# Samples' attention over a paged cache: queries spread by GpSimd copies, a page over 64 partitions, page tables loaded ahead

## The chip, the core and the metric

The kernel runs on one core of one Trainium2 chip. Its time is the device time of one execution in microseconds (us), as the median of several runs. A core has a matmul engine (TensorE, PE in the rows), a vector engine (VectorE, DVE), an activation engine (ScalarE, ACT), a general one (GpSimd, POOL) and a queue engine (SyncE, SP) that issues most DMAs. Each runs its own list of instructions in order, and they meet at semaphores. SPq and ACTq in the rows are the instructions that issue DMAs.

## The reference

One step of a two-layer decoder: a convolution layer and an attention layer, both with an MLP, for one prompt of 512 tokens and eight samples of eight tokens. All is float32. The change touches the samples' attention in the second layer, which reads a cache of latents and rotary keys through a table of pages:

```python
past_c = cache_kv_latent[page_table].reshape(DB, past_len, KV_LORA)      # 8 samples, 2048 keys, 512
past_kr = cache_k_rope[page_table].reshape(DB, past_len, QK_ROPE)        # 64
...
def sample_attention(q_lat, q_rope, past_c, past_kr, c, kr):
    s_past = latent_scores(q_lat, q_rope, past_c, past_kr)
    s_new = latent_scores(q_lat, q_rope, c, kr)
    s_new = jnp.where(jnp.tril(jnp.ones((T, T), dtype=bool)), s_new, -jnp.inf)
    p = jax.nn.softmax(jnp.concatenate([s_past, s_new], axis=-1), axis=-1).astype(c.dtype)
    return (jnp.einsum('bqhk,bkc->bqhc', p[..., :P], past_c)
            + jnp.einsum('bqhk,bkc->bqhc', p[..., P:], c))
```

A sample has 16 pages of 128 keys; eight heads of eight tokens make 64 queries.

## The kernel before, in words

The work on the two groups goes on together until the prompt's attention is done (eight heads, `hd`, with four blocks of queries each). Then comes the stage in question: a loop over the eight samples `i`. A sample is two units `u` = 2i and 2i + 1 of eight pages, and a unit two halves `s` of four pages.

**Loads.** `cache_loads` is SP's program. A unit's latents go to one of four places in `HELD` (`half_pages`), its ropes to one of four in `ROPES`; so unit u can be loaded only when unit u - 4 has been read (`unit_read`). Page `q` of a half goes to partitions 32q to 32q + 31, four keys in each (8 KB of latents, 1 KB of ropes): per unit 8 + 8 DMAs, ordered latents, ropes, latents, ropes by half. `pages_of` loads a sample's row of the page table into `table` by a DMA and waits for it; `page(n)` reads one number of it into a register (`value_load`, L490). Units 0 to 3 are loaded in code that is written out and has its own waits for buffers of the stage before; units 4 to 15 in a loop `Fori(1, NS // 2)` over pairs of samples. Both DMAs of a half raise one semaphore (`half_landed`).

**Turning.** DVE transposes blocks of 32x32, so that the channels lie on the partitions: `turn_pages` (L2376, half a unit) and `turn_ropes` (L2382, half a unit) into `TURN[u % 2]`, that is `TURNED` or `Y`.

**Queries.** The scores read `Q4[0]`: 18 blocks of 64 queries by 32 channels on partitions, each of the four 32-partition groups with the channels in another order. `QLAT` and `QRS` hold all samples' queries. `queries(i)`, on ACT, copies sample i's by 18 DMAs: 16 from 32 partitions of `QLAT` to 32 others (L1394), two for the ropes (L1396). Sample 0's go into `Q4[0]`, all others into `Q4[1]`, and GpSimd copies `Q4[1]` to `Q4[0]` (L1752) when the sample before has been scored. GpSimd also copies the queries for the new keys to `QS` (L1747, L1749).

**The order in a sample.** PE's `sequence`: scores of unit u (L3092 from `TURNED`) and of u + 1 (L3092 from `Y`), turning the weights (`turn`, L3099), `give` (L3127, the sample before), values of u (L3112), turn, the swap (L3153), the new keys of the next sample (L3080, L3082), values of u + 1. ACT's: `weigh` of the sample before (L1423), `weights` (the exponentials, L1430) and `turned_weights` (L1445) for u and u + 1, then `queries(i + 2)`. DVE's: `unit_top(u)` (L2405), pages of u + 2, `unit_top(u + 1)`, ropes of u + 2, half the pages of u + 3, `unit_sum` (L2417, L2420), `keep`, `gain_output(u)` (L2428), the rest of u + 3, `finish` (L2440 to L2453; its L2446 waits for ACT's L1423), `new_top(i + 1)` (L2391, L2393), for which PE's second scores wait.

**Sample 0.** At the end of the prompt's last head PE waits for `q4_in`, sample 0's 18 DMAs, before its new keys (L3080), since these read the ropes from `Q4[0]`; behind them in PE's list stand the last head's turn (L3053, after DVE's L2338, after ACT's L1368, after DVE's L2329) and its output (L3063). ACT issues the DMAs before that L1368. After the stage PE goes on with the products of `wo` (L2557).

Of the kernel before, what the change touches and what calls it, by code (L numbers as in the profile page):

```python
# [39 lines left out]
NS, TQ = 8, 8  # L40
# [221 lines left out]
def decoder_step(nc, io):  # L262
    with ExitStack() as ctx:
# [168 lines left out]
        CHUNKS = 4  # L432
        OUTS = 3
        MERGES = 5
        Q4_LOADS = 18
# [12 lines left out]
        def half_ropes(u, s):  # L448

            return ROPES[u % 4][:, 256 * s:256 * s + 256]  # L450
# [7 lines left out]
        table_in, keys_turned, score_mm, unit_read, q4_in, csn_mm = (  # L458
            sem("table_in"), sem("keys_turned"), sem("score_mm"), sem("unit_read"), sem("q4_in"), sem("csn_mm"))
# [12 lines left out]
        table = sb("table", [1, PAGES], I32)  # L472
# [3 lines left out]
        def half_landed(u, s):  # L476

            return pages_in[u % 4][s], 128 * (u // 4 + 1)

        def cache_loads(sp):  # L480

            def pages_of(sample):

                sp.dma_start(table[:], io["page_table"][sample, :]).then_inc(table_in, 16)
                sp.wait_ge(table_in, 16)
                sp.sem_clear(table_in)
# [5 lines left out]
            def load_latents(u, s, pages):  # L492

                dst = half_pages(u, s).rearrange("p (a c) -> p a c", a=1)
# [5 lines left out]
            def load_ropes(u, s, pages):  # L500

                dst = half_ropes(u, s).rearrange("p (a c) -> p a c", a=1)
                for q in range(4):
                    sp.dma_start(dst[32 * q:32 * q + 32],  # L504
                                 io["cache_k_rope"].rearrange("n (p k) c -> p n (k c)", k=4)[:, bass.ds(pages[q], 1)])\
                        .then_inc(half_landed(u, s)[0], 16)

            pages_of(slice(0, 1))
# [3 lines left out]
            pages = [page(q) for q in range(16)]  # L512
            for s in range(2):
                load_latents(0, s, pages[4 * s:4 * s + 4])
            sp.wait_ge(kvt_done, NH)
            sp.wait_ge(v_mm, NH // 2)
            for s in range(2):
                load_ropes(0, s, pages[4 * s:4 * s + 4])
            for s in range(2):
                load_latents(1, s, pages[8 + 4 * s:12 + 4 * s])  # L520
                load_ropes(1, s, pages[8 + 4 * s:12 + 4 * s])
            pages_of(slice(1, 2))
            pages = [page(q) for q in range(16)]
            for s in range(2):
                load_latents(2, s, pages[4 * s:4 * s + 4])
            sp.wait_ge(pe_read_raw, 4)
            for s in range(2):
                load_latents(3, s, pages[8 + 4 * s:12 + 4 * s])
            sp.wait_ge(s_mm, 4 * NH)
            for s in range(2):  # L530
                load_ropes(2, s, pages[4 * s:4 * s + 4])
            sp.wait_ge(pv_mm, NH)
            for s in range(2):
                load_ropes(3, s, pages[8 + 4 * s:12 + 4 * s])
            with sp.Fori(1, NS // 2) as i:
                for e in range(2):
                    pages_of(bass.ds(2 * i + e, 1))
                    for k in (2 * e, 2 * e + 1):
                        pages = [page(8 * (k % 2) + q) for q in range(8)]
                        sp.wait_ge(unit_read, 4 * i + k - 3)  # L540
                        sp.wait_ge(ones_set, 1)
                        for s in range(2):
                            load_latents(k, s, pages[4 * s:4 * s + 4])
                            load_ropes(k, s, pages[4 * s:4 * s + 4])
# [270 lines left out]
        def _(act):  # L815
# [573 lines left out]
            def queries(i):  # L1389

                dst = Q4[1 if i else 0]
                for m in range(4):
                    for a in range(4):
                        act.dma_start(dst[32 * a:32 * a + 32, 4 * m:4 * m + 4], QLAT[32 * m:32 * m + 32, i]).then_inc(q4_in, 16)  # L1394
                for r in range(2):
                    act.dma_start(dst[:, 16 + r], QRS[r][:, 64 * i:64 * i + 64]).then_inc(q4_in, 16)  # L1396

            head_keys(0)
            for hd in range(NH):
# [12 lines left out]
                else:  # L1412
                    act.wait_ge(ql_used, NH)
                    act.wait_ge(qrs_c, 2)
                    queries(0)
# [36 lines left out]
            act.wait_ge(s_mm, 4 * NH)  # L1452
            queries(1)
            for i in range(NS):
# [6 lines left out]
                if i < NS - 2:  # L1461
# [1854 lines left out]
```

## Time and profile before

| | us |
|---|---|
| runs: median of 3 (lowest to highest) | 1846.39 (1844.89 to 1852.63) |
| the profiled execution: its time | 1851.93 |
| its span | 1850.2 |
| busy in the span: PE, POOL, DVE, ACT | 1683.0, 980.1, 927.8, 681.9 |
| from the first scores of sample 0 to the first product of `wo` | 240.8 |

The span is what the profile covers, from the first instruction to the last; 1.7 us lie around it. Starts are in us from the span's start. A row of a timeline has a start, a length that runs from the first to the last of its xN instructions, the engine, the line, the operation and in brackets how long the engine stood idle before it and what ended that. "issue" is time in which the engine waited for nothing that the profile shows, such as its own sequencer at other instructions.

### The profile page before, as it was taken

To read this page: it belongs to the slowest core of one execution; us is meant where nothing else is said; L and a number is where in the kernel's file an instruction comes from. 1 tells how busy PE (TensorE), PEld (TensorE's weight loads), DVE (VectorE), ACT (ScalarE), POOL (GpSimd) and SP (SyncE) were. 2 spreads that over 40 slices of the span, in tenths; PEclk is the share of its full clock that TensorE was granted. 3 is DMA by queue.
4 is the path that set the end of the run, shared out by engine and by line. 5 is a ranking of instruction groups with operands and counts; after the bars stand their busy time and mean duration, and the time that the engine had idled before them with its cause. 6 is when DMAs were issued, how large, how long until landed. Compare 5 with 4: busy or idle time off the path is not lost.

```text
span 1850.2 us, 39735 instructions
## 1 busy us (share of the span) xinstructions
PE 1683.0 (91%) x15818; PEld 1562.7 (84%) x15818; DVE 927.8 (50%) x2134; ACT 681.9 (37%) x1296; POOL 980.1 (53%) x823
## 2 busy tenths in 40 slices
PE   7998899999999999999998388578999999999998
PEld 6997799988999999989766255355989999999988
DVE  5897799844224556662655354544162222222283
ACT  5565444453454544532232011102242222322342
POOL 4994799966899966744110000000645455554652
PEclk9998999999999999999999789778999999999999
DMA  7322355543445532223004557865612322222201
GB/s 211 102 81 61 128 171 171 160 140 124 141 157 182 160 114 77 70 52 122 1 1 103 128 119 166 176 147 130 204 44 86 91 91 91 68 78 81 92 24 52
DMA packets 167835, 203.43 MB, mean 110 GB/s; under 512 B 21034, under 2 KB 134276, under 8 KB 163603
## 3 DMA queue, kind: packets, MB, share of 16 engines
q1 hardware_dynamic: 155150, 194.28, 36.5%
q10 hardware_dynamic: 12548, 7.41, 1.7%
q8 instruction: 76, 1.25, 0.3%
q14 instruction: 61, 0.49, 0.1%
HBM read 192.14 MB, written 4.79 MB: 106 GB/s over the span
## 4 chain that ended last, share of the span: by engine, by line
PE 63%; POOL 11%; DVE 9%; SPq 6%; issue 5%; DMA 3%; ACT 2%; ACTq 1%; POOLq 0%; DVEq 0%
PE bank L2557 19%; PE bank L2559 18%; PE bank L2558 18%; POOL WL L1509 4%; SPq L490 2%; SPq L504 2%; SPq L496 2%; POOL WL L1507 2%; POOL acc L1534 1%; POOL R L1572 1%; PE bank L3063 1%; PE bank L3092 1%; POOL root L1572 1%; DMA table<-in_page_table 1%; DVE bank L1807 1%
## 5 line engine op out<-in xcount | busy, mean ns | idle before, releaser
L1509 POOL TENSOR_TENSOR WL<-RAW,WH 128x1024 fp32r<-128x1024 f32 (+3 forms) x279 | 575.0, 2069 | 256.8 <-ACT WH L825 255.1
L2557 PE MATMUL bank<-AH,WH 128*128 128x288 f32 x2080 | 626.6, 301 | 30.1 <-DVE AL L1779 13.4
L2558 PE MATMUL bank<-AL,WH 128*128 128x288 f32 x2080 | 617.4, 297 | 0.0
L2559 PE MATMUL bank<-AH,WL 128*128 128x288 f32 x2080 | 617.2, 297 | 0.0
L2557 PEld LDWEIGHTS bank<-AH,WH 128*128 128x128 f32 x2080 | 394.7, 190 | 41.6 <-DVE AL L1779 16.1
L2558 PEld LDWEIGHTS bank<-AL,WH 128*128 128x128 f32 x2080 | 395.2, 190 | 0.7
L2559 PEld LDWEIGHTS bank<-AH,WL 128*128 128x128 f32 x2080 | 395.0, 190 | 0.0
L825 ACT ACTIVATE WH<-RAW 128x1024 fp32r<-128x1024 f32 (+1 forms) x281 | 291.9, 1045 | 264.6 <-PE bank L2559 264.2
L2557 PE MATMUL bank<-BH,WH 128*128 128x288 f32 (+1 forms) x1120 | 337.0, 301 | 13.8 <-DVE S L1828 4.1
L2559 PE MATMUL bank<-BH,WL 128*128 128x288 f32 (+1 forms) x1120 | 333.5, 298 | 0.0
L2558 PE MATMUL bank<-BL,WH 128*128 128x288 f32 (+1 forms) x1120 | 333.4, 298 | 0.0
L2557 PEld LDWEIGHTS bank<-BH,WH 128*128 128x128 f32 x1120 | 210.5, 188 | 19.2 <-issue 15.2
L2559 PEld LDWEIGHTS bank<-BH,WL 128*128 128x128 f32 x1120 | 210.6, 188 | 1.4
L2558 PEld LDWEIGHTS bank<-BL,WH 128*128 128x128 f32 x1120 | 210.6, 188 | 1.3
L1507 POOL TENSOR_TENSOR WL<-RAW,WH 128x256 fp32r<-128x256 f32 (+2 forms) x135 | 119.6, 907 | 163.6 <-ACT WH L825 163.6
L1904 DVE SCALAR_TENSOR_TENSOR bank<-S,taps,bank 128x224 f32<-128x224 f32 x464 | 134.6, 364 | 0.0
L2105 DVE TENSOR_TENSOR prod<-R,bank 128x288 f32<-128x288 f32 x64 | 29.0, 454 | 176.9 <-ACT R L1175 100.5
L2114 DVE TENSOR_TENSOR Y<-Y,bank 128x288 f32<-128x288 f32 x112 | 50.7, 453 | 110.2 <-PE bank L2559 110.2
L1534 POOL TENSOR_TENSOR acc<-acc,sq 128x288 f32<-128x288 f32 x97 | 78.4, 814 | 32.8 <-ACT sq L843 28.1
L1747 POOL COPY S<-S 128x256 f32<-128x256 f32 x7 | 2.8, 402 | 161.5 <-PE bank L3082 81.8
L1681 POOL TENSOR_TENSOR BL<-prod,BH 128x288 fp32r<-128x288 f32 x64 | 51.4, 809 | 67.1 <-ACT BH L1179 67.1
L3112 PE MATMUL bank<-HELD,root 128*64 128x512 f32 x256 | 75.2, 676 | 0.2
(308 smaller groups left out, 2076.6 us busy)
## 6 DMA issues: line engine op xcount, KB each, us to landing
RAW<-in_w_up SPq DMA_DIRECT2D x48, 1024.0 KB, 5.5
RAW<-in_w_down SPq DMA_DIRECT2D x48, 1024.0 KB, 5.2
HELD<-in_cache_kv_latent SPq DMA_DIRECT2D x128, 256.0 KB, 5.3
RAW<-in_conv_pw SPq DMA_DIRECT2D x16, 512.0 KB, 7.2
RAW<-in_conv_pw SPq DMA_DIRECT2D x8, 1024.0 KB, 5.2
RAW<-in_ple_gate SPq DMA_DIRECT2D x8, 1024.0 KB, 5.2
S<-S ACTq DMA_DIRECT2D x136, 32.0 KB
RAW<-in_w_o SPq DMA_DIRECT2D x4, 1024.0 KB, 7.5
```

Of the source, the lines that this page charges most:

```text
L490: return sp.value_load(table[0:1, n:n + 1], min_val=0, max_val=io["cache_kv_latent"].shape[0] - 1)
L825: nc.scalar.activation(split_part(WH, d, q), raw_part(d, q), ACT.Copy).then_inc(hi_done, 1)
L1507: nc.gpsimd.tensor_tensor(dst[:, 0:a], src[:, 0:a], hi[:, 0:a], ALU.subtract)
L1509: nc.gpsimd.tensor_tensor(dst, src, hi, ALU.subtract).then_inc(lo_done, 1)
L1534: nc.gpsimd.tensor_tensor(dst, dst, src, ALU.add).then_inc(acc_done, 1)
L1681: nc.gpsimd.tensor_tensor(half(BL, m, h), prod[:, n % 2, :], half(BH, m, h).bitcast(F32), ALU.subtract).then_inc(u_lo, 1)
L1904: nc.vector.scalar_tensor_tensor(out=run if c < CW - 1 else out, in0=src, scalar=w, in1=run, op0=ALU.mult, op1=ALU.add).then_inc(conv_late, 1)
L2114: nc.vector.tensor_tensor(half(Y, m, h), half(Y, m, h), bank[u % BANKS][:, 0:H], ALU.add)\
L2557: nc.tensor.matmul(out, wh, xh, start=first, stop=False)
L2558: nc.tensor.matmul(out, wh, xl, start=False, stop=False)
L2559: return nc.tensor.matmul(out, wl, xh, start=False, stop=last)
L3112: ins = nc.tensor.matmul(dst[g], SPT[:, k * P + 64 * g:k * P + 64 * g + 64], half_pages(u, g)[:, k * CL:(k + 1) * CL], start=k == 0 and (j ...
```

## The change

1. **Queries.** `queries` goes. `stage_queries(i)` on GpSimd makes the same 16 copies of 32 partitions in four groups of four, with a wait behind each group, and two of 128 partitions. Sample 0's are staged once `ql_used` and `qrs_c` allow, sample 1's once the prompt's scores are done, and those of i + 1 right behind the copy of `Q4[1]` to `Q4[0]`. PE's new keys of sample 0 read `QRS` and don't wait for `q4_in`.
2. **Pages.** Page n goes over 64 partitions (n even: 0 to 63, n odd: 64 to 127) with two keys in each, 4 KB of latents and 512 bytes of ropes; still eight DMAs of latents and eight of ropes a unit, now all latents first. Ropes have semaphores of their own (`ropes_landed`), so pages are turned before them, and `turn_ropes` turns a whole unit at once (`CHUNKS` 4 to 3).
3. **Tables.** `table` has two rows; a sample's is loaded while the one two before it is in use. Units 4 to 15 are written out in place of the loop, and `unit_read` is waited for behind the page numbers as before.
4. **DVE.** `new_top(i + 1)` stands ahead of `finish(i)`; sample 0's rope turns stand behind the last `norm`.

```diff
-        CHUNKS = 4
+        CHUNKS = 3
...
-            def page(n):
-
-                return sp.value_load(table[0:1, n:n + 1], min_val=0, max_val=io["cache_kv_latent"].shape[0] - 1)
...
-                for q in range(4):
-                    sp.dma_start(dst[32 * q:32 * q + 32],
-                                 io["cache_kv_latent"].rearrange("n (p k) c -> p n (k c)", k=4)[:, bass.ds(pages[q], 1)])\
-                        .then_inc(half_landed(u, s)[0], 16)
...
+            def pages_of(u):
+
+                i = u // 2
+                if u % 2 == 0:
+                    sp.wait_ge(table_in[i % 2], 16 * (i // 2 + 1))
+                    sp.wait_ge(ones_set, 1)
+                at = u % 4 * 8
+                pages = [sp.value_load(table[0:1, at + n:at + n + 1], min_val=0,
+                                       max_val=io["cache_kv_latent"].shape[0] - 1) for n in range(8)]
+                if u % 2 and i + 2 < NS:
+                    load_table(i + 2)
+                return pages
...
+                for n in range(8):
+                    rows64, at = slice(64 * (n % 2), 64 * (n % 2) + 64), n % 4 // 2 * 2 * CL
+                    dst = half_pages(u, n // 4).rearrange("p (a c) -> p a c", a=1)[rows64, :, at:at + 2 * CL]
+                    sp.dma_start(dst, io["cache_kv_latent"].rearrange("n (p k) c -> p n (k c)", k=2)[:, bass.ds(pages[n], 1)])\
+                        .then_inc(half_landed(u, n // 4)[0], 16)
...
+            for u in range(4, UNITS2):
+                pages = pages_of(u)
+                sp.wait_ge(ones_set, 1)
+                sp.wait_ge(unit_read, u - 3)
+                load_latents(u, pages)
+                load_ropes(u, pages)
...
-            def queries(i):
-
-                dst = Q4[1 if i else 0]
-                for m in range(4):
-                    for a in range(4):
-                        act.dma_start(dst[32 * a:32 * a + 32, 4 * m:4 * m + 4], QLAT[32 * m:32 * m + 32, i]).then_inc(q4_in, 16)
-                for r in range(2):
-                    act.dma_start(dst[:, 16 + r], QRS[r][:, 64 * i:64 * i + 64]).then_inc(q4_in, 16)
...
+            def stage_queries(i):
+
+                dst = Q4[1 if i else 0]
+                for d in range(4):
+                    for m in range(4):
+                        a = (m + d) % 4
+                        nc.gpsimd.tensor_copy(dst[32 * a:32 * a + 32, 4 * m:4 * m + 4], QLAT[32 * m:32 * m + 32, i])\
+                            .then_inc(q4_staged, 1)
+                    pool.wait_ge(q4_staged, Q4_PARTS * i + 4 * d + 4)
+                for r in range(2):
+                    nc.gpsimd.tensor_copy(dst[:, 16 + r], QRS[r][:, 64 * i:64 * i + 64]).then_inc(q4_staged, 1)
...
                 if more:
                     turn_pages(u + 3, 1)
-                    turn_ropes(u + 3, 0)
-                    turn_ropes(u + 3, 1)
+                    turn_ropes(u + 3)
+                    new_top(i + 1)
                 finish(i)
-                if more:
-                    new_top(i + 1)
...
-            pe.wait_ge(q4_in, 16 * Q4_LOADS)
-            new_keys([QLAT[:, 0, c, :] for c in range(4)] + [Q4[0][:, 16 + r, :] for r in range(2)])
+            new_keys([QLAT[:, 0, c, :] for c in range(4)] + [QRS[r][:, 0:64] for r in range(2)])
```

What stands in an engine's list before and after, at two places. First ACT in one sample of the loop, before: values' weights, the 18 DMAs, and `weigh` (S<-S 128x2).

```order
L1430 ACTIVATE prod,S<-bank,S 128x4x4x32
L1437 ACTIVATE S<-S 128x1
L1445 ACTIVATE root<-bank 128x512
L1394 DMA S<-S 32x256 x16
L1396 DMA S<-S 128x64
L1396 DMA S<-R 128x64
L1423 ACTIVATE S<-S 128x2
```

GpSimd in one sample, after: the copies to `QS`, `Q4[1]` to `Q4[0]` (128x1152), and the new ones.

```order
L1752 COPY S<-S 128x256
L1754 COPY S<-S 128x64
L1754 COPY S<-R 128x64
L1757 COPY S<-S 128x1152
L1735 COPY S<-S 32x256 x16
L1739 COPY S<-S 128x64
L1739 COPY S<-R 128x64
```

ACT's three rows of DMAs are gone in the changed kernel, where L1415, its `weigh`, follows L1437 directly; they are GpSimd's last three rows here.

Second, DVE at the end of a sample's turning, before: `gain_output(u)`, the last turns (`Y`), `finish`, `new_top`, and the top of the next sample.

```order
L2428 COPY S<-bank 128x512
L2376 STREAM_TRANSPOSE Y<-HELD 128x4x16x32
L2382 STREAM_TRANSPOSE Y<-S 128x4x2x32 x2
L2440 COPY S<-bank 128x2
L2441 COPY S<-S 128x2
L2443 TENSOR_TENSOR S<-S 128x1
L2431 SCALAR_TENSOR_TENSOR S<-S,bank 128x512
L2446 TENSOR_SCALAR S<-S 128x1
...
L2453 TENSOR_SCALAR scaled<-scaled,S 128x64
L2391 TENSOR_TENSOR S<-bank,taps 64x64
L2393 TENSOR_REDUCE S<-S 64x1
L2405 TENSOR_REDUCE S<-bank 128x1
```

The same place after:

```order
L2436 COPY S<-bank 128x512
L2384 STREAM_TRANSPOSE Y<-HELD 128x4x16x32
L2390 STREAM_TRANSPOSE Y<-S 128x8x2x32
L2399 TENSOR_TENSOR S<-bank,taps 64x64
L2401 TENSOR_REDUCE S<-S 64x1
L2448 COPY S<-bank 128x2
L2449 COPY S<-S 128x2
L2451 TENSOR_TENSOR S<-S 128x1
L2439 SCALAR_TENSOR_TENSOR S<-S,bank 128x512
L2454 TENSOR_SCALAR S<-S 128x1
...
L2413 TENSOR_REDUCE S<-bank 128x1
```

The two rows of `new_top` moved ahead of `finish`, whose fifth row (now L2454) waits for ACT, and one rope turn stands where two did.

## Rows read from the trace of the kernel before

**Rows 1.** The page's 40 slices: PE's busy share in tenths.
```profile
PE   7998899999999999999998388578999999999998
```

**Rows 2.** Stretches by sample: length, busy of each engine, PEclk, DMA share, GB/s.
```profile
1085.16:1111.71 26.55, 22.30 (x643) 16.02 (x641) 15.70 (x26) 3.55 (x11) 1.91 (x4) 0.87 0.76 169
...
1274.80:1294.74 19.94, 19.92 (x642) 13.68 (x641) 5.48 (x18) 7.18 (x15) 2.90 (x3) 1.00 0.32 105
```

**Rows 3.** PE in order of time, from the last head of the prompt on.
```profile
1044.09 1.09 PE L3080 MATMUL bank<-S 128*64 128x64 f32 x8 [24.33 <-DMA S<-R]
...
1046.39 1.06 PE L3053 MATMUL bank<-ident,scaled 128*128 128x128 f32 x4
...
1053.90 6.08 PE L3092 MATMUL bank<-TURNED,S 32*64 32x128 f32 x288 [3.34 <-DVE scaled L2502]
...
1073.66 6.23 PE L3112 MATMUL bank<-HELD,root 128*64 128x512 f32 x15
...
1093.74 6.62 PE L3092 MATMUL bank<-Y,S 32*64 32x128 f32 x288 [4.25 <-DVE S L2391]
...
1111.71 4.31 PE L3092 MATMUL bank<-TURNED,S 32*64 32x128 f32 x288
...
1129.73 4.01 PE L3112 MATMUL bank<-HELD,root 128*64 128x512 f32 x15
...
1202.91 0.59 PE L3153 MATMUL bank<-S,scaled 128*128 128x2 f32 x2 [6.02 <-DVE S L2420]
```

**Rows 4.** ACT and DVE in order of time, at the same places.
```profile
1018.51 9.70 ACTq L1394 DMA_DIRECT2D S<-S  x15
...
1022.65 0.15 DVE L2329 TENSOR_SCALAR tiny<-tiny 128x1 f32<-128x1 f32 x1
...
1029.61 0.69 ACT L1368 ACTIVATE scaled<-bank,tiny 128x512 f32<-128x512 f32 x1 [10.84 <-issue]
...
1030.69 0.49 DVE L2338 TENSOR_SCALAR scaled<-scaled,tiny 128x512 f32<-128x512 f32 x1
...
1092.09 0.29 ACT L1423 ACTIVATE S<-S 128x2 f32<-128x2 f32 x1 [10.98 <-issue]
```

**Rows 5.** SP's DMA issues in order of time: start, length, line, destination and source.
```profile
0.75 1.82 SPq L623 DMA_DIRECT2D Y<-in_x_prompt  x4
...
1023.71 9.02 SPq L496 DMA_DIRECT2D HELD<-in_cache_kv_latent  x16
...
1080.09 1.82 SPq L496 DMA_DIRECT2D HELD<-in_cache_kv_latent  x4
...
1179.08 1.83 SPq L496 DMA_DIRECT2D HELD<-in_cache_kv_latent  x4
...
1191.51 1.82 SPq L496 DMA_DIRECT2D HELD<-in_cache_kv_latent  x4
...
1257.00 1.82 SPq L496 DMA_DIRECT2D HELD<-in_cache_kv_latent  x4
```

**Rows 6.** SP's waits: us in total, times, longest, 960 to 1300.
```profile
SPq L486 <- DMA table<-in_page_table: 23.5, 7, 5.5
```

**Rows 7.** The chain of waits through SP's queue: start, us, what.
```profile
1200.34 6.17 issue
```

**Rows 8.** DMA issues in the stage: count, KB each, median us to landing.
```profile
HELD<-in_cache_kv_latent SPq DMA_DIRECT2D x128, 256.0 KB, 5.3
```

**Rows 9.** GpSimd's copies in the stage, shapes apart: busy us, mean ns.
```profile
L1752 POOL COPY S<-S 128x1152 f32<-128x1152 f32 x7 | 8.1, 1151 | 107.8 <-PE bank L3092 107.8
L1747 POOL COPY S<-S 128x256 f32<-128x256 f32 x7 | 2.8, 402 | 161.5 <-PE bank L3082 81.8 <-PE bank L3063 79.7
L1749 POOL COPY S<-R 128x64 f32<-128x64 f32 x7 | 1.7, 238 | 0.0
```

**Rows 10.** Two stretches: weight loads, then page loads; columns as in rows 2.
```profile
506.00:552.00 46.00, 46.00 (x348) 46.00 (x347) 9.82 (x22) 23.17 (x40) 43.06 (x32) 1.00 0.50 161
...
1000.00:1012.00 12.00, 7.71 (x49) 5.93 (x47) 7.83 (x17) 3.30 (x8) 0.00 (x0) 1.00 1.03 224
```

More of the change, by code:

```diff
@@ L457, in decoder_step @@
         pt_mm, pt_used, pv_mm = sem("pt_mm"), sem("pt_used"), sem("pv_mm")
[L458 to L459 removed]
+        table_in, keys_turned, score_mm, unit_read, q4_staged, csn_mm = (
+            [sem(f"table_in{e}") for e in range(2)], sem("keys_turned"), sem("score_mm"), sem("unit_read"), sem("q4_staged"),
+            sem("csn_mm"))
+        ropes_in = [sem(f"ropes_in{k}") for k in range(4)]
         pages_in = [[sem(f"pages_in{k}{h}") for h in range(2)] for k in range(4)]
@@ L500, in load_ropes, with load_table @@
[L500 to L508, printed above, removed]
+            def load_table(i):
+                sp.dma_start(table[0:1, i % 2 * PAGES:(i % 2 + 1) * PAGES], io["page_table"][i:i + 1, :])                    .then_inc(table_in[i % 2], 16)
@@ new lines, in load_latents, with load_ropes @@
+            def load_latents(u, pages):
+                for n in range(8):
[3 more added lines that the diff above has]
+                        .then_inc(half_landed(u, n // 4)[0], 16)
+            def load_ropes(u, pages):
+                for n in range(8):
+                    rows64, at = slice(64 * (n % 2), 64 * (n % 2) + 64), n // 2 * 2 * DR
+                    dst = unit_ropes(u).rearrange("p (a c) -> p a c", a=1)[rows64, :, at:at + 2 * DR]
+                    sp.dma_start(dst, io["cache_k_rope"].rearrange("n (p k) c -> p n (k c)", k=2)[:, bass.ds(pages[n], 1)])\
+                        .then_inc(ropes_landed(u)[0], 16)
@@ L511, in cache_loads @@
             sp.wait_ge(pe_read_raw, 3)
-            pages = [page(q) for q in range(16)]
-            for s in range(2):
-                load_latents(0, s, pages[4 * s:4 * s + 4])
+            pages = pages_of(0)
+            load_latents(0, pages)
             sp.wait_ge(kvt_done, NH)
             sp.wait_ge(v_mm, NH // 2)
[L517 to L525, printed above, removed]
+            load_ropes(0, pages)
+            pages = pages_of(1)
+            load_latents(1, pages)
+            load_ropes(1, pages)
+            pages = pages_of(2)
+            load_latents(2, pages)
+            late = pages_of(3)
+            sp.wait_ge(ones_set, 1)
             sp.wait_ge(pe_read_raw, 4)
-            for s in range(2):
-                load_latents(3, s, pages[8 + 4 * s:12 + 4 * s])
+            load_latents(3, late)
             sp.wait_ge(s_mm, 4 * NH)
-            for s in range(2):
-                load_ropes(2, s, pages[4 * s:4 * s + 4])
+            load_ropes(2, pages)
             sp.wait_ge(pv_mm, NH)
[L533 to L544, printed above, removed]
+            load_ropes(3, late)
+            for u in range(4, UNITS2):
+                pages = pages_of(u)
+                sp.wait_ge(ones_set, 1)
+                sp.wait_ge(unit_read, u - 3)
+                load_latents(u, pages)
+                load_ropes(u, pages)
         @block.sync
```

60 lines of the change are left out of this document (27 added, 33 removed).

## Prediction

> **What bounds the kernel now.** I first read the page's slices. The matmul engine is busy for nine tenths or more nearly everywhere; one dip of six slices stands in the middle [rows 1]. It is the sample group's attention over the paged cache, from about 1,016 us to 1,294.74 us. Nothing outside it is touched, so everything below is about that stretch.
>
> Then the stretches by sample. The second sample takes 26.55 us, the shortest, and the matmul engine works 22.3 us of it; later ones take 32.2 on average by the loads of units 4 to 15 (176.9 / 5.5 [rows 5]). From the scores of the last sample on it has no gaps (19.92 of 19.94) [rows 2]. So the stage is bound by what PE waits for. The instructions in order of time tell it apart into three waits. (a) Before sample 0, PE stands 24.33 us on a DMA, the last of ACT's 18 copies of the queries [rows 3]. (b) In the first samples it waits about 4.25 us for DVE's L2391, and DVE waits for ACT's L1423, which was held for 10.98 us of "issue": ACT was issuing the next sample's 18 query DMAs [rows 3, 4]. (c) Later it waits some 6 us a sample for DVE's L2420 [rows 3], which stands in DVE's list behind turns of the next pages.
>
> For (c) the SP queue has to be read. From unit 4's first load at 1080.09 to unit 15's at 1257.00 SP never stops because a buffer is in use; it is busy with its own work. An undisturbed unit takes 1191.51 - 1179.08 = 12.43 us: 16 DMAs of which four take 1.83, and eight loads of page numbers [rows 5]. Eleven such units would be 136.7 us; they took 176.9. The rest is the wait for the page table (23.5 us in 7 waits [rows 6], of which five lie here, one for each of samples 3 to 7), "issue" at the loop's jump back (6.17 us at the second of two [rows 7]), and slower issuing while ACT issues too.
>
> **The change, part by part, against the profiled execution** (span 1850.2, itself 1851.93 us, with the median of the runs at 1846.39; I subtract from the median).
>
> 1. Sample 0's queries. PE's new-key products no longer wait for a DMA, since they read QLAT and QRS directly, and ACT doesn't issue. What is late next is the last head of the prompt: DVE's L2329 ended at 1022.80, ACT took it up at 1029.61 after 10.84 us of issue, and DVE's L2338 ended at 1031.18. Without the issue these are 6.8 us earlier, so 1024.4. PE's L3053 needs only that, and ran at 1046.39 [rows 3, 4]. Gain 22.0. The cover is GpSimd's staging: it can begin where ACT's DMAs did, one issue before 1018.51, at 1017.9, and the scores now start at 1053.90 - 22.0 = 1031.9, so 18 copies have 14.0 us, 0.78 each. No row shows GpSimd copying 32 partitions to other partitions. The nearest is 128x256 at 402 ns, the same elements per partition; the ends are 238 ns (64 elements) and 1151 ns (1,152) [rows 9]. I take 402 ns: 16 x 0.40 + 2 x 0.24 = 6.9 us, hidden. At the upper end 20.7 us, which costs 6.7 here.
>
> 2. The first sample. After a long stop PE's scores took 6.08 us and its values 6.23, against 4.31 and 4.01 later [rows 3]; PE now stops for only a few us. Gain between 0 and 4.0; I take 2.0. Unit 4's load waits for unit 0 to be read: 1080.09 - 24.0 = 1056.1. SP is ready by then: units 2 and 3's latents are issued by 1032.7 before and have the same work ahead of them after [rows 5]; 16 rope loads (8.0) and unit 4's page numbers (12.43 - 8.0 = 4.4) end at 1045.1.
>
> 3. The loads. Per unit there are still 16 DMAs and eight page-number loads; tables are loaded two samples ahead, so their waits go, and the loop is written out, so the jumps go. A table load's issue stays, about 0.5 us in two units. The disputed price is that of issuing a DMA over 64 partitions in place of 32: rows show 1.83 for four over 32, and 1.82 for four over 128 partitions [rows 5], so I take no change. 11 x (12.43 + 0.25) = 139.5 in place of 176.9. Gain 37.4. Lower end: a DMA at the 0.65 us that ACT's took (9.70 for 15 [rows 4]), 16 x 0.15 = 2.4 more in a unit, 26 in all, leaves 11. Upper end: the matmul engine takes over as the bound (below).
>
> The transfers lie beside this. A unit is 8 x (256 + 32) KB = 2.36 MB. With the DMA engines full, page loads ran at 224 GB/s, weight loads at 161 GB/s with a share of 0.50, so some 320 GB/s when full [rows 10]. At 224 a unit takes 10.5 us, under 12.7; at 320, 7.4. Either is hidden; I take 10.5, as the packets stay 4 KB and the loads still take turns over halves of the partitions. [...]
>
> 4. ACT gets 18 issues a sample back, 11.5 us (18 x 0.64), and DVE does new_top before finish: wait (b) is gone. It is worth nothing by itself in most samples, since the loads are later, but it keeps PE's own limit down: 26.55 - 4.25 = 22.3 us a sample, against 2 x 12.68 = 25.4 for the loads. GpSimd's work in a sample becomes 6.9 + 2.0 us of 25.4.
>
> 5. The tail. From unit 15's first load to the first wo product it took 1294.74 - 1257.00 = 37.74 us. The first transpose now needs four DMAs and not eight to be issued, 2.2 us less [rows 5]; transfers take 5.3 us [rows 8] and the same bytes wait before them, so I count 1.2 (0 to 2.2). The merged rope transpose is the same elements in half the instructions: nothing.
>
> Sum: 22.0 + 2.0 + 37.4 + 1.2 = 62.6. In times: scores at 1031.9, unit 4 at 1056.1, unit 15 at 1195.6, wo at 1232.1. 1846.4 - 62.6 = 1783.8 us.
>
> **Rivals.**
> - Loads stop being the bound. Then PE's own work does: 1031.9 + 29.3 for sample 0 (1085.16 - 1053.90, less the 2.0), 6 x 22.3, and 19.9 give wo at 1214.9, so 1767. It needs SP under 11.2 us for a unit, which no row shows; but half the gap could come from a shorter page-number load. Chance 0.07.
> - SP's issue is dearer: 0.65 a DMA, or the written-out code has to be fetched. Something like fetching is seen at a jump, 6.17 us [rows 7]; if such a stop came for each 128 or so instructions of SP's 900, seven of them would cost up to 43. With half of the first or a few of the second, 15 to 27 us of the 37 are lost: 1799 to 1811. Against it: SP's written-out first part, issued without a gap. Chance 0.2.
> - Pages over 64 partitions at 4 KB transfer slower. Below 186 GB/s (2.36 MB in 12.7 us) the transfer binds; at 170, 13.9 us a unit, 13 us lost: 1797. Chance 0.06, and covered by the range.
> - Slower than before: GpSimd's copies across partitions. The queries of eight samples, 144 copies, must be staged before sample 7's scores, and with 7 x 2.0 us of its other copies they fill the 256.9 us from 1017.9 to 1274.80 at 1.69 us a copy. That is the point from which it decides; at 1.8 the kernel takes 1862 us. For it: no such copy stands in the trace, and GpSimd's shared working with DVE's transposes isn't shown. Against it: it is four times the row of its size and above the row of 4.5 times its size. Chance 0.04. [...]
> - The change doesn't do what it says, for instance PE finds another late releaser, such as new_top waiting for the new keys: then sample periods stay near 28 us. 7 x 2.6 = 18 lost: 1802. Chance 0.08.
>
> **Chances and range.** The forecast, 1775 to 1793, has 0.55; the rivals 0.07, 0.2, 0.06, 0.04, 0.08. The range 1766 to 1807 holds the first, the forecast, the transfer rival, the last, and most of the second. A measurement of this kernel can tell about 0.5%, 9 us, from no change. Faster by more than that takes all but the slower rival and a heavy mix of two others: 0.93; the same 0.03; slower 0.04.
>
> **What would show it.** PE's 24.33 us before L3080 gone, and the first scores near 1032. GpSimd's 32x256 copies near 0.4 us. No DMA on ACT's queue in the stage, and its L1423 without issue. In SP's queue a unit every 12.4 to 12.9 us, without gaps at the table or a jump. PE still waiting 2 to 4 us a sample for L2420's successor behind a transpose. The DMA share of the stage near 0.85. I am wrong if SP's pitch in a unit is over 13.5 us, if SP waits for unit_read in most units, or if GpSimd releases PE's scores.

## The result, and the profile after

| | before | after |
|---|---|---|
| median of the runs, us (lowest to highest) | 1847.08 (1844.89 to 1852.63) | 1824.24 (1822.48 to 1828.44) |
| the profiled execution: time, span | 1851.93, 1850.2 | 1824.45, 1822.6 |
| from the first scores of sample 0 to the first product of `wo` | 240.8 | 234.8 |

The ratio is 0.9875 with a 95% interval of 0.9848 to 0.9903: faster by some 23 us. 1783.8 had been forecast, with a range of 1766 to 1807, so the direction was right, the size was about a third of the 62.6 us forecast, and the time lies outside the range. The dip in the page's slices of PE, the counterpart of [rows 1], has a lowest slice of 6 in place of 3, and is about as wide as it was:

```profile
PE   7998899998999999999899688688989999999998
```

PE in order of time, with the first sample's scores and, further down, the wait for the swap of a later sample (columns as in [rows 3]):

```profile
1031.55 4.81 PE L3095 MATMUL bank<-TURNED,S 32*64 32x128 f32 x175 [3.49 <-DVE scaled L2509]
1037.11 1.88 PE L3095 MATMUL bank<-TURNED,S 32*64 32x128 f32 x113 [0.75 <-issue]
...
1044.52 3.72 PE L3095 MATMUL bank<-Y,S 32*64 32x128 f32 x128 [5.06 <-issue]
1048.55 2.62 PE L3095 MATMUL bank<-Y,S 32*64 32x128 f32 x128 [0.31 <-issue]
1052.55 0.65 PE L3095 MATMUL bank<-Y,S 32*64 32x128 f32 x19 [1.39 <-issue]
...
1208.95 0.59 PE L3156 MATMUL bank<-S,scaled 128*128 128x2 f32 x2 [8.61 <-DVE S L2428]
```

The 24.33 us before the new keys are gone, and the first scores begin at 1031.55 in place of 1053.90. But the swap, which waited 6.02 us for DVE in the row of before [rows 3], now waits 8.61. Who waits there is DVE's turning, for the latents:

```profile
DVE Y L2384 <- DMA HELD<-in_cache_kv_latent: 38.8, 10, 7.6
PE bank L3156 <- DVE S L2428: 38.8, 5, 8.8
```

(The waits from 1060 to 1230: us in total, times, longest.) So the pace is SP's, as before. Its issues in order of time, the first two units of the written-out part and the last:

```profile
1059.91 5.09 SPq L510 DMA_DIRECT2D HELD<-in_cache_kv_latent  x8
1065.18 5.03 SPq L518 DMA_DIRECT2D HELD<-in_cache_k_rope  x8
1074.68 0.25 SPq L490 DMA_DIRECT2D table<-in_page_table  x1
1075.18 5.05 SPq L510 DMA_DIRECT2D HELD<-in_cache_kv_latent  x8
...
1229.51 5.16 SPq L510 DMA_DIRECT2D HELD<-in_cache_kv_latent  x8
```

From unit 4 to unit 15 it takes 169.60 us, 15.42 a unit. No table is waited for, no jump stands in it, and SP waits for no unit to be read behind unit 4; but eight DMAs over 64 partitions take 5.03 to 5.16 us mostly, where four over 32 took 1.83 [rows 5]. The stretch as one row, columns as in [rows 2]: PE works 130.61 of 169.60 us, and the DMA engines have room.

```profile
1059.91:1229.51 169.60, 130.61 (x3844) 90.41 (x3842) 90.14 (x140) 21.40 (x64) 47.18 (x121) 0.86 0.69 153
```

GpSimd's copies across partitions, which no row of before showed, took 397 ns each, and its large copy is unchanged (L1757, 1152 ns beside 1151 in [rows 9]):

```profile
L1735 POOL COPY S<-S 32x256 f32<-32x256 f32 x128 | 50.8, 397 | 52.2 <-DVE R L2358 44.6 <-POOL S L1739 0.2
```

### The profile page after: what moved, and what is told of

Same layout as the page of the kernel before. It is cut to its first block, busy times and chain, and to the rows that moved or that the text cites. A ratio compares the mean times of both kernels' runs of the same rounds, so it can differ in the third digit from the quotient of the medians.

```text
span 1822.6 us, 39699 instructions
## 1 busy us (share of the span) xinstructions
PE 1680.8 (92%) x15818; PEld 1561.1 (86%) x15818; DVE 926.7 (51%) x2118; ACT 682.0 (37%) x1296; POOL 1034.8 (57%) x967
## 4 chain that ended last, share of the span: by engine, by line
PE 65%; DVE 10%; POOL 9%; SPq 8%; issue 5%; ACT 3%; DMA 1%; POOLq 0%; DVEq 0%; ACTq 0%
PE bank L2560 20%; PE bank L2562 19%; PE bank L2561 19%; POOL WL L1496 4%; SPq L510 3%; SPq L518 3%; SPq L499 2%; PE bank L3095 1%; PE bank L3066 1%; POOL R L1559 1%; POOL root L1559 1%; POOL WL L1494 1%; DVE bank L1815 1%; PE bank L3115 1%; DVE AL L1787 1%
## 5 line engine op out<-in xcount | busy, mean ns | idle before, releaser
L2560 PEld LDWEIGHTS bank<-AH,WH 128*128 128x128 f32 x2080 | 395.3, 190 | 40.4 <-DVE AL L1787 15.4
L830 ACT ACTIVATE WH<-RAW 128x1024 fp32r<-128x1024 f32 (+1 forms) x281 | 291.6, 1045 | 264.2 <-PE bank L2562 263.9
L1735 POOL COPY S<-S 32x256 f32<-32x256 f32 x128 | 50.8, 397 | 52.2 <-DVE R L2358 44.6
L3115 PE MATMUL bank<-HELD,root 128*64 128x512 f32 x256 | 75.3, 678 | 0.2 <-issue 0.2
```

The costliest lines, as they stand in the source:

```text
L830: nc.scalar.activation(split_part(WH, d, q), raw_part(d, q), ACT.Copy).then_inc(hi_done, 1)
L2560: nc.tensor.matmul(out, wh, xh, start=first, stop=False)
L3115: ins = nc.tensor.matmul(dst[g], SPT[:, k * P + 64 * g:k * P + 64 * g + 64], half_pages(u, g)[:, k * CL:(k + 1) * CL], start=k == 0 and (j ...
```

## Experiments

Theory A: issuing one DMA over 64 partitions occupies SP for about 0.15 us more than one over 32, 16 times a unit, in a stretch that SP bounds. Rival B: something else of the change slows SP: the written-out code, the ropes' own semaphores, or the latents all first. Every run below stood beside runs of the kernel before whose median was 1850.88 us (`e_after_p32`, `e_after_p128`, `b_p64`, `e_probe`), 1850.99 (`b_q`, `e_p32_plain`, `e_p128_plain`, `e_late3`) or 1852.75 (`e_p32_tab`, `e_p32_fin`, `e_after_plain`, `e_probe2`). That is 4 to 6 us above the median of the result, so kernels are compared by their ratios to the kernel before, and by times in their profiled executions.

### The part undone: a page over 32 partitions, and over 128

`e_after_p32`, the changed kernel with 32 partitions a page (the ropes alike):

```diff
-                    rows64, at = slice(64 * (n % 2), 64 * (n % 2) + 64), n % 4 // 2 * 2 * CL
+                    rows, at = slice(32 * (n % 4), 32 * (n % 4) + 32), n % 4 // 4 * 4 * CL
...
-                    sp.dma_start(dst, io["cache_kv_latent"].rearrange("n (p k) c -> p n (k c)", k=2)[:, bass.ds(pages[n], 1)])\
+                    sp.dma_start(dst, io["cache_kv_latent"].rearrange("n (p k) c -> p n (k c)", k=4)[:, bass.ds(pages[n], 1)])\
```

> The changed kernel with one part undone: a page again over 32 partitions with four keys each, all else as changed. Theory A (a DMA over 64 partitions costs SP about 0.15 us more to issue than one over 32: 0.66 against 0.50 us with what lies between, 468 against 316 ns of the instruction): four DMAs take 1.83 us, a unit 12.4 to 12.9 us, 11 units about 139 in place of 169.6 us, so up to 30 us less than the changed kernel: 1795 us, or a few us more if DVE's chain comes next. Theory B (what slows SP is the written-out code, the ropes' own semaphores or the order of the latents): the unit stays near 15.4 us and the time at 1824 us.

`e_after_p128` is the same with `k=1` and all 128 partitions:

> The changed kernel with a page over all 128 partitions, one key each, so packets of 2 KB and 256 bytes in place of 4 KB and 512. Theory A1 (64 partitions are dear by themselves, 32 and 128 cheap, as four DMAs over 128 partitions took 1.82 us early in the kernel before): four DMAs take 1.8 to 2.0 us, a unit 12.5 to 13.5 us, 1795 to 1803 us, unless transfers in 2 KB packets take over 13 us a unit (then SP waits for units to be read). Theory A2 (the price rises with the count of partitions): over 0.66 us a DMA, a unit over 15.4 us, slower than 1824 us. Theory B: the unit stays near 15.4 us.

And `b_p64` is the kernel before with `k=2` and 64 partitions, and nothing else:

> The kernel before with only a page over 64 partitions, two keys each, in the place of 32. Theory A: each of the 16 DMAs of a unit costs 0.15 us more, an undisturbed unit 14.9 in place of 12.43 us, 11 units about 26 us more: 1873 us. Theory B (the spread costs nothing, the loop and its order matter): 1847 us within 5 us.

| | median, us | ratio to before (95%) | unit 4 to unit 15, us |
|---|---|---|---|
| before | | 1 | 176.9 |
| `b_p64` | 1861.97 | 1.0062 (1.0039 to 1.0085) | 194.0 |
| after | 1824.24 | 0.9875 (0.9848 to 0.9903) | 169.6 |
| `e_after_p32` | 1796.48 | 0.9706 (0.9689 to 0.9722) | 141.7 |
| `e_after_p128` | 1796.72 | 0.9702 (0.9686 to 0.9719) | 145.3 |

The instruction itself, from the instructions that write `HELD` behind 1,060 us (shortest, median and longest in ns): before, after, `e_after_p32`, `e_after_p128` and `b_p64` in that order.

```profile
L496 SPq DMA_DIRECT2D HELD<-in_cache_kv_latent x96: 315/316/490, 1080.1 to 1262.8; - x96
```
```profile
L510 SPq DMA_DIRECT2D HELD<-in_cache_kv_latent x96: 468/468/583, 1059.9 to 1234.2; - x96
```
```profile
L510 SPq DMA_DIRECT2D HELD<-in_cache_kv_latent x95: 315/316/324, 1060.1 to 1204.8; - x95
```
```profile
L510 SPq DMA_DIRECT2D HELD<-in_cache_kv_latent x95: 332/333/358, 1059.8 to 1208.2; - x95
```
```profile
L497 SPq DMA_DIRECT2D HELD<-in_cache_kv_latent x96: 468/469/634, 1074.5 to 1276.2; - x96
```

The instruction takes 316 ns over 32 partitions, 468 over 64 and 333 over 128. All else is kept but the bytes in each partition, which fall as the count rises (8, 4 and 2 KB); the probes further down hold them at 256. Theory A holds, in its form that 64 alone is dear, and B falls: with the written-out code, the semaphores and the order kept, a unit takes 12.88 us (141.7 / 11). The 64 partitions cost 27.9 us there (169.6 - 141.7), 16 x 11 DMAs at 0.152 being 26.8.

`b_p64` was sized wrongly by A: 26 us were expected and the ratio gives 11. The units lost 17.1 us, as the DMAs' 26.8 are partly given back by shorter waits for the page table, 15.2 us in 7 in place of 23.5 [rows 6]; of these, the five between unit 4 and unit 15 total 11.5 us in place of 17.0. And sample 0's queries arrived sooner: PE waited 16.33 us for them, not 24.33 [rows 3], and the first scores began at 1048.35, 5.5 us sooner. 17.1 less 5.5 is 11.6, and the medians lie 11.1 us apart.

```profile
SPq L486 <- DMA table<-in_page_table: 15.2, 7, 3.7
```
```profile
1036.37 1.08 PE L3080 MATMUL bank<-S 128*64 128x64 f32 x8 [16.33 <-DMA S<-R]
```

Both are small transfers that stood behind page loads, and pages issued more slowly let them through sooner. That reading of the two rows was not tested by itself.

### Which counts of partitions are dear

Behind unit 15's loads of the changed kernel, 32 extra DMAs of 256 bytes a partition in eight groups of four:

```diff
+            place = half_pages(13, 0).rearrange("p (a c) -> p (a c)", a=1)
+            for k, (start, rows) in enumerate([(0, 32), (0, 64), (64, 64), (0, 128), (0, 16), (0, 48), (0, 96), (0, 120)]):
+                for j in range(4):
+                    at = (4 * k + j) * 64
+                    sp.dma_start(place[start:start + rows, at:at + 64], io["cache_kv_latent"][0, start:start + rows, 0:64])\
+                        .then_inc(probed, 16)
+                sp.wait_ge(probed, 64 * (k + 1))
```

> The changed kernel with 32 extra DMAs behind unit 15's, each 256 bytes a partition from one fixed page into a place that has been read: four each over partitions 0 to 31, 0 to 63, 64 to 127, 0 to 127, 0 to 15, 0 to 47, 0 to 95 and 0 to 119, with a wait behind each four. Theory A1: the instruction takes about 316 ns over 32 and 330 to 350 over 128 and 120 partitions, about 470 over 64, at either start. Theory A2: it rises with the count of partitions, so over 500 ns at 128. Theory B: all the same within 50 ns.

`e_probe2` has another list: (0, 64), (0, 65), (0, 63), (32, 64), (0, 56), (0, 80), (0, 112), (0, 8).

> The changed kernel with 32 extra DMAs behind unit 15's, four each over 64 partitions from 0, 65 from 0, 63 from 0, 64 from 32, 56, 80, 112 and 8 from 0, 256 bytes a partition. In the first such kernel 64 took 597 ns at either start, and 16, 32, 48, 96, 120 and 128 took 374 to 430. Theory P (only a count of just 64 is dear): 597 for the first and the fourth, 370 to 430 for all others. Rival Q (a range around 64, or every count that isn't a multiple of 16 or 32, is dear): 63, 65 or 56 and 80 also over 500.

The first four groups of `e_probe` (0 to 31, 0 to 63, 64 to 127, 0 to 127), then the first four of `e_probe2` (0 to 63, 0 to 64, 0 to 62, 32 to 95):

```profile
L557 SPq DMA_DIRECT2D HELD<-in_cache_kv_latent x4: 332/412/423, 1248.0 to 1249.3; - x4
...
L557 SPq DMA_DIRECT2D HELD<-in_cache_kv_latent x4: 512/596/597, 1250.9 to 1252.8; - x4
...
L557 SPq DMA_DIRECT2D HELD<-in_cache_kv_latent x4: 465/597/597, 1254.9 to 1256.7; - x4
...
L557 SPq DMA_DIRECT2D HELD<-in_cache_kv_latent x4: 366/430/432, 1258.7 to 1260.1; - x4
```
```profile
L557 SPq DMA_DIRECT2D HELD<-in_cache_kv_latent x4: 486/589/597, 1245.0 to 1246.8; - x4
...
L557 SPq DMA_DIRECT2D HELD<-in_cache_kv_latent x4: 342/364/372, 1248.7 to 1249.9; - x4
...
L557 SPq DMA_DIRECT2D HELD<-in_cache_kv_latent x4: 273/324/332, 1251.6 to 1252.7; - x4
...
L557 SPq DMA_DIRECT2D HELD<-in_cache_kv_latent x4: 581/592/594, 1254.2 to 1256.1; - x4
```

A count of exactly 64 is dear, wherever it starts: 589 to 597 ns, with 63 at 324 and 65 at 364. Medians for 16, 48, 96 and 120 partitions were 420, 416, 374 and 393. The single instructions took 331 to 389 ns over 56, 322 to 422 over 80, 312 to 430 over 112 and 277 to 295 over 8; none over another count than 64 took more than 432. Theory P holds. With 256 bytes a partition and a fixed address, the instructions over 32, 64 and 128 take some 0.1 us more than in the kernel's own loads. The step at 64 is 0.17 to 0.18 us over 32 and 128, about as in the kernel, and 0.23 to 0.27 over 65 and 63. Why that count costs more stays open.

### One part alone: the queries; and the tables undone

`b_q` is the kernel before with `stage_queries` on GpSimd in place of `queries` on ACT, and PE's new keys as after:

```diff
-            pe.wait_ge(q4_in, 16 * Q4_LOADS)
-            new_keys([QLAT[:, 0, c, :] for c in range(4)] + [Q4[0][:, 16 + r, :] for r in range(2)])
+            new_keys([QLAT[:, 0, c, :] for c in range(4)] + [QRS[r][:, 0:64] for r in range(2)])
```

> The kernel before with the queries alone changed: GpSimd copies them as in the changed kernel, ACT issues no DMAs and PE's new keys of sample 0 read QLAT and QRS. Theory: the 24.33 us before sample 0's new keys go, the first scores start near 1032 (22 us earlier), and 20 to 26 us of the median go: 1825 to 1831 beside a kernel before of 1851. Rival (the copies only pay together with the new order of loads, since SP's unit 4 and its tables set the pace): under 15 us.

`e_p32_tab` is `e_after_p32` with each table loaded where it is needed (the first two at the start are gone too):

```diff
                 if u % 2 == 0:
+                    load_table(i)
                     sp.wait_ge(table_in[i % 2], 16 * (i // 2 + 1))
...
-                if u % 2 and i + 2 < NS:
-                    load_table(i + 2)
```

> The kernel e_after_p32 with the tables' part undone: each sample's row of the page table is loaded by SP where its first unit begins, and waited for at once. Theory (a wait of 2 to 5.5 us stands in each of samples 3 to 7 on SP's list, as in the kernel before and in b_q): 10 to 22 us slower than e_after_p32's 1796: 1806 to 1818 beside a kernel before of 1851; the rest of the distance to b_q (1828) is the loop's jumps and the order on DVE. Rival (the written-out code alone gave the gain): within 5 us of 1796.

`b_q` took 1827.98 us, a ratio of 0.9884 (0.9867 to 0.99), 23.0 us under its kernel before. Its first scores start at 1035.46, 18.4 us sooner than before and not 22. The gain is nearly the whole gain of the change: everything else in it came to nothing, since the 64 partitions took away what the rest gave. `e_p32_tab` took 1820.07 us, 0.9833 (0.9811 to 0.9855). Its waits for the table:

```profile
SPq L500 <- DMA table<-in_page_table: 30.5, 7, 5.0
```

By ratios, in shares of a kernel before of 1851 us: the queries give 21 us (1 - 0.9884), the written-out loop and the order of DVE and ropes 9 (0.9884 - 0.9833), the tables ahead 24 (0.9833 - 0.9706), and 64 partitions take 31 (0.9875 - 0.9706). With these intervals each share is good to some 5 us, so the 9 is the least certain. The expectation for the tables, at most 22, was a little low: the waits there total 30.5 us in 7.

### The first sample

The prediction gave 2.0 us for a faster first sample; it became 2.2 us slower. Its scores stop for 0.75, 5.06, 0.31 and 1.39 us of "issue" (above), with no engine to wait for. Before, they stopped for 1.50, 1.94 and 1.65, the last two of which are

```profile
1065.96 2.08 PE L3092 MATMUL bank<-Y,S 32*64 32x128 f32 x128 [1.94 <-issue]
1069.70 0.65 PE L3092 MATMUL bank<-Y,S 32*64 32x128 f32 x19 [1.65 <-issue]
```

Around the longest stop of after, from 1039.47 to 1044.52, the DMA engines were full or nearly so, with the pages of units 2 and 3 under way (columns as in [rows 2]):

```profile
1036.00:1040.00 4.00, 2.70 (x149) 1.98 (x133) 0.94 (x3) 0.01 (x1) 0.00 (x0) 0.99 1.02 236
1040.00:1044.00 4.00, 0.00 (x0) 0.00 (x0) 4.00 (x2) 1.10 (x4) 0.00 (x0) 0.86 0.80 169
1044.00:1048.00 4.00, 3.48 (x128) 3.32 (x128) 0.37 (x1) 0.00 (x0) 0.00 (x0) 0.50 0.16 38
```

`e_late3` holds unit 3's latents, and what stands behind them, until unit 0 is scored:

```diff
+            sp.wait_ge(score_mm, 1)
             load_latents(3, late)
```

> The changed kernel with unit 3's latents, and the ropes of units 2 and 3 behind them, held back until unit 0 has been scored. Theory F (the matmul engine's stops of 0.75, 5.06, 0.31 and 1.39 us of issue in the first scores are waits for its own instructions, which are fetched behind page loads that run at a DMA share near 1): with fewer pages under way between 1032 and 1039 us the stop of 5.06 us shrinks to 1.5 to 2 or moves behind the loads that now start at about 1037, as they then fill the engines at another of the stops. Rival (the stops have nothing to do with the loads): 0.75, 5.06, 0.31 and 1.39 us within 0.3 us.

```profile
1030.74 6.44 PE L3096 MATMUL bank<-TURNED,S 32*64 32x128 f32 x288 [3.45 <-DVE scaled L2510]
...
1038.72 2.08 PE L3096 MATMUL bank<-Y,S 32*64 32x128 f32 x128 [1.11 <-issue]
1044.11 2.66 PE L3096 MATMUL bank<-Y,S 32*64 32x128 f32 x128 [3.31 <-issue]
1050.31 1.11 PE L3096 MATMUL bank<-Y,S 32*64 32x128 f32 x19 [3.54 <-issue]
```
```profile
1037.42 6.16 SPq L510 DMA_DIRECT2D HELD<-in_cache_kv_latent  x8
1043.76 10.74 SPq L518 DMA_DIRECT2D S<-in_cache_k_rope  x16
```

With fewer pages under way the first unit's scores run through in 6.44 us, and the next stop is 1.11. The loads then start at 1037.42, and now the last two stops are 3.31 and 3.54 in place of 0.31 and 1.39. The sum is the same (7.96 against 7.51 us), and so is the time, 1825.78 in one run. That fits theory F in its second form, but one profile is thin. `e_probe` and `e_probe2` have the code of after up to unit 15's loads, and their stops total 8.19 and 5.32 us; in `e_probe2` too the first unit's scores run through, in 6.58 us, with the loads about where they were in after.

More weight lies in all the traces together. Each stop of over 3 us (in after, `b_q`, `e_after_p32`, `e_p32_tab`, `e_late3` and `e_probe`, 3.31 to 5.41 us) stands in a stretch with a DMA share of 0.60 to 1.02. Where the pages went over 128 partitions, the transfers were done sooner: in `e_after_p128` the share is 0.10 from 1,043 to 1,047 us, and its stops are 1.22, 1.67 and 1.65, no longer than before. So long stops come with busy DMA engines, and their size under the same loads varies by some 3 us. That the stops are fetches of PE's own instructions is argued, not shown. Two things fit: they stand only in the first of a loop's passes through this code (in after the next sample's first 288 products run through in 4.30 us, from 1065.03), and the profile shows a queue of the kind "instruction" at work in after from 1,045 to 1,056 us (packets, MB, share).

```profile
q8 instruction: 3, 0.05, 2.2%
```

### What bounds it next

If SP's list is the bound, cheaper page numbers must help as much as cheaper DMAs. A page number is three instructions on SP in the changed kernel: the load, the arithmetic of a test of its bounds and the assertion. The plain form leaves the test out; the numbers and what is computed stay the same as long as the table is valid.

```profile
L499 SPq TENSOR_LOAD <-table x88: 261/266/659, 1070.3 to 1228.8; - x88
L499 SPq FUSED_REGOPS  x88: 147/147/159, 1070.6 to 1229.1; - x88
L499 SPq SEQ_ASSERT  x88: 18/18/18, 1070.8 to 1229.3; - x88
```

```diff
-                pages = [sp.value_load(table[0:1, at + n:at + n + 1], min_val=0,
-                                       max_val=io["cache_kv_latent"].shape[0] - 1) for n in range(8)]
+                pages = [sp.value_load(table[0:1, at + n:at + n + 1]) for n in range(8)]
```

`e_after_plain` is the changed kernel with that edit, `e_p32_plain` and `e_p128_plain` are `e_after_p32` and `e_after_p128` with it, and `e_p32_fin` is `e_p32_plain` with `new_top(i + 1)` behind `finish(i)` again.

> The changed kernel itself with the page numbers loaded without the test of their bounds, 64 partitions kept. Theory (SP's own list is the bound there, and its terms add up): a unit is 10.8 + 16 x 0.155 = 13.3 us in place of 15.4, 11 units 23 us less: 1801 beside a changed kernel of 1824. Rival (something behind the issue, as the transfers of 64-partition pages, binds at 15.4): 1824 still.

> The kernel e_after_p32 (32 partitions a page) with the page numbers loaded without the test of their bounds: 8 loads of 0.27 us and little else in a unit in place of 4.9 us. If SP's own list still sets the pace there, a unit goes from 12.88 to about 11.2 us, where the matmul engine's 22.3 us a sample takes over, and the time from 1796 to 1778. If its transfers bind (2.36 MB at 224 GB/s is 10.5 us a unit, with stops for buffers more), 1780 to 1787. If DVE's chain binds, it stays near 1796.

> The kernel e_after_p128 (a page over 128 partitions) with the page numbers loaded without the test of their bounds. A unit's issue is 8 x 0.50 + 8 x 0.50 + 2.4 = about 10.6 us; its transfers ran at over 300 GB/s when the DMA engines were full, 7.6 us a unit, so only PE's work binds: 1778 us or a few less. If the time is clearly under e_p32_plain's, transfers bind in that one.

> The kernel e_p32_plain (32 partitions, page numbers without their test) with the order on DVE undone: new_top behind finish again. Theory: with ACT no longer issuing DMAs, finish's wait for ACT is short, and new_top lies 2 us later in a stretch where PE's second scores come 4 us after: within 5 us of e_p32_plain's 1771. Rival (the order is what keeps PE near its limit): 7 samples of 1 to 2.5 us, 1778 to 1788.

| | median, us | ratio to before (95%) | a unit on SP, us |
|---|---|---|---|
| `e_after_plain` | 1800.40 | 0.9716 (0.9694 to 0.9737) | 13.32 |
| `e_p32_plain` | 1770.93 | 0.9570 (0.9554 to 0.9586) | 10.82 |
| `e_p128_plain` | 1772.45 | 0.9569 (0.9548 to 0.9590) | 11.14 |
| `e_p32_fin` | 1769.53 | 0.9554 (0.9535 to 0.9573) | 10.82 |

`e_after_plain` came out at a unit of 13.32 us where 13.3 was expected: SP's terms add up, and the rival that something behind the issue holds the unit at 15.4 us falls. `e_p32_plain` is the fastest version with `e_p128_plain` and `e_p32_fin`, 80 us or 4.3% under the kernel before and 3% under the changed one, and it is 7 us faster than expected. I had held its unit to 11.2 us by PE's 22.3 us a sample; it went to 10.82, which makes 4 of the 7. PE's own work in a sample is less than the 22.3 us: that row [rows 2] has a granted clock of 0.87. Here, at 1.00, the third sample's scores start 19.96 us after the second's, as the last sample of before took 19.94. Later samples follow SP at 2 x 10.82.

```profile
1064.98 4.31 PE L3094 MATMUL bank<-TURNED,S 32*64 32x128 f32 x288
...
1084.94 4.31 PE L3094 MATMUL bank<-TURNED,S 32*64 32x128 f32 x288
```

DVE's order is worth nothing there (0.9554 against 0.9570, with intervals that overlap), as the prediction had it; in the changed kernel itself it was not tested alone. The partitions decide how full the DMA engines are, at the same time: `e_p32_plain` and then `e_p128_plain`, 1,060 to 1,180 us.

```profile
1060.00:1180.00 120.00, 114.70 (x3810) 79.84 (x3812) 86.67 (x137) 20.29 (x61) 43.69 (x113) 0.99 0.98 217
```
```profile
1060.00:1180.00 120.00, 112.29 (x3663) 78.94 (x3666) 80.68 (x128) 19.53 (x60) 42.95 (x110) 0.96 0.66 211
```

217 GB/s fill them with 32 partitions a page, and 211 take two thirds of them with 128, so 128 could carry some 320 by an estimate (211 / 0.66). Over 32 partitions the transfers, PE (114.70 of 120 us) and SP all stand near their limits at once. The two kernels take the same time, so the fuller engines cost nothing that the runs show. Why the same bytes fill less of their time over 128 partitions, no run shows. Over 32, a unit's loads go over the four quarters, one DMA behind the other, and they stayed at 217 GB/s.

## Why the prediction was wrong, point by point

| step | forecast, us | measured, by the profiled executions, us |
|---|---|---|
| 1. sample 0's queries | 22.0 | 22.35 (1053.90 - 1031.55) |
| 2. the first sample | 2.0 | -2.2 (26.19, now 28.36) |
| 3. units 4 to 15 | 37.4 | 7.3 (176.9, now 169.6) |
| 4. ACT freed, DVE's order | 0 | DVE's order 0 (`e_p32_fin`); ACT freed not measured alone |
| 5. the tail | 1.2 | 0.9 (37.74, now 36.85) |
| sum | 62.6 | 28.4 (`wo` at 1294.74, now 1266.36) |

The medians differ by 22.8, not 28.4, since the profiled execution of before lay 5.5 us over the median from which I subtracted.

**Right:** what bounds the kernel, and where: SP's own list in units 4 to 15. The scores at 1031.9 (1031.55), GpSimd's copy at 402 ns (397), no DMA on ACT, no wait for a table, no jump, SP never waiting for `unit_read` behind unit 4, and DVE still releasing the swap. One of the prediction's signs of being wrong came true: SP's pitch in a unit, 15.42 us, is over 13.5. The tables and the written-out loop gave what was worked out: over 32 partitions 11 units took 141.7 us, where 139.5 had been expected.

**Right in part by luck: term 1.** The scores came within 0.4 us of the forecast, but two things that it didn't have cancel in the 22.35. PE came to the last head's turns 2.2 us sooner than before, for which no run gives the cause, and then the eight products of that head's output took 4.63 us at a granted clock of 0.50, where they took 2.42 at 1.00 before. Before and then after:

```profile
1016.51 0.38 PE L3053 MATMUL bank<-ident,scaled 128*128 128x128 f32 x2
...
1048.13 2.42 PE L3063 MATMUL bank<-S,root 128*128 128x512 f32 x8 [0.69 <-ACT S L1379]
```
```profile
1014.35 0.38 PE L3056 MATMUL bank<-ident,scaled 128*128 128x128 f32 x2
...
1023.42 4.63 PE L3066 MATMUL bank<-S,root 128*128 128x512 f32 x8 [0.69 <-ACT S L1384]
```

From the first of these rows to the first scores it took 37.39 us before and 17.20 after. So from there on the change gave 20.2 us, in line with the 21 of `b_q`.

**The step that failed is one price in term 3:** "rows show 1.83 for four over 32, and 1.82 for four over 128 partitions [rows 5], so I take no change". Two rows on either side of a count were taken to bound what lies between. They do not: 64 costs 468 ns, above both 316 and 333. The trace of before had DMAs over just 64 partitions outside the stage, and I argued from the neighbours without looking for them. The line behind the four issues that [rows 5] quotes from the kernel's start is one, a load of the samples' 64 rows (0.59 us alone, where four over 128 take 1.82), and so is the samples' part of `p`, whose instructions take 512 ns where those for the prompt's 128 rows take 433 (medians of 2 and 8):

```profile
2.62 0.59 SPq L626 DMA_DIRECT2D S<-in_x_sample  x1
```
```profile
L617 SPq DMA_DIRECT2D S<-in_p_sample x2: 488/512/536, 372.1 to 1313.1; - x2
```

The lower end of that term had the right size, "16 x 0.15 = 2.4 more in a unit, 26 in all, leaves 11", from ACT's issues over 32 partitions, and the rival that "SP's issue is dearer" reached 1811. But I gave it 0.2, and ended the range at 1807, inside that rival, though the bounds of this cost alone go to 1810. With 27.9 us lost to it and 4.2 to the first sample the sum is 62.6 - 27.9 - 4.2 = 30.5, hence 1816; the rest of the way to 1824 is mostly the 5.5 us by which the profiled execution of before lay over the median. That "the packets stay 4 KB" was a wrong reading, since a page over 32 partitions has 8 KB of latents in each and one over 64 has 4. It cost nothing: at 153 GB/s and a DMA share of 0.69 the transfers had room.

**Term 2 had the wrong sign.** Its step from PE's slow scores and values to a gain failed: the values became as fast as forecast (15 products of L3115 in 4.01 us, where 6.23 before), but the scores' products became 2.8 us slower. The mean granted clock of the first sample is 0.80 in both kernels, in rows of before and of after,

```profile
1053.90:1080.09 26.19, 21.09 (x609) 14.57 (x610) 11.75 (x15) 2.66 (x9) 1.15 (x1) 0.80 0.11 27
```
```profile
1031.55:1059.91 28.36, 20.68 (x610) 15.81 (x611) 11.87 (x13) 2.66 (x9) 5.87 (x13) 0.80 0.42 96
```

and PE works about as long (21.09 and 20.68). The DMA share grew, 0.11 to 0.42: starting the scores 22 us sooner put PE's first pass through its code on top of the page loads of units 2 and 3. And the stops for issue grew from 5.1 us (1.50, 1.94 and 1.65 before) to 7.5, 2.4 more, against 2.2 lost. The stops are thus what made the stretch longer; that the loads made the stops longer fits the traces (above) and was not isolated. What the values won was lost again behind the stop of 5.06 us: the granted clock there is 0.50 (1,044 to 1,048), and 128 products take 3.72 us in place of 2.08 at 1.00 (the row at 1065.96).

**The rival of PE as the bound** was placed at 1767 and would need "SP under 11.2 us for a unit, which no row shows". `e_p32_plain` reached 10.82 us and 1770.9. PE waits there only 6.5 us in 4 for the swap, from 1,060 to 1,230 us.

## What to carry to other kernels

Where a queue engine's own list is the bound, every instruction in it has a price, and it is to be read from a row of the very shape: here one count of partitions costs half as much again as those around it (468 ns beside 316 and 333), and a test of bounds costs half as much as a DMA (2.1 us in eight, 0.26 each, beside 0.50). Before a shape is changed, look through the whole trace for that shape, at any place, rather than for its neighbours. And a change that starts a stage earlier also moves it onto other traffic: ask what ran beside the old place and what runs beside the new one. Last, a term that came out as forecast is to be taken apart too, before it is called right.

## What the runs showed of the hardware that I had not expected

- Issuing a DMA from SP over exactly 64 partitions takes 468 ns in place of 316 (32) or 333 (128); with 256 bytes a partition 589 to 597, against 324 over 63 and 364 over 65. Starting at partition 0, 32 or 64 made no difference (589 to 597, 592, 597).
- A page number with its test of bounds takes 266 + 147 + 18 ns and what lies between, and without the test a unit with its eight numbers is 2.1 us shorter (15.42 to 13.32).
- The same bytes in pages over 128 partitions fill two thirds of the DMA engines' time, over 32 nearly all (0.66 at 211 GB/s, 0.98 at 217).
- GpSimd copies 32x256 elements to other partitions in 397 ns, the same as a 128x256 copy in place (402 [rows 9]).
- PE stops in its first pass through the scores' code (5.1 us in three stops before, 7.5 in four after). Stops of 3.31 to 5.41 us stood only where the DMA share was 0.60 or more; with the engines nearly idle they were 1.5 to 1.94 us (before, a share of 0.11 over that sample). The cause is not isolated.
